# 66 TensorE passes of several shapes behind the last transposes of a hybrid decoder step

## The reference

```
proj = rmsnorm(x) @ w_in               # q, k, v, indexer, S5 input, two gates
y_a  = sparse_attention(...) @ w_attn_proj
y_b  = glu(gelu(s5_scan(u)) @ w_glu)
x    = x + (sigmoid(ga) * y_a + sigmoid(gb) * y_b) @ w_out
up   = rmsnorm(x) @ w_up               # 2 x 5632 columns
a    = silu(gate) * val                # after a causal depthwise conv of width 3
x    = x + a @ w_down
y    = rmsnorm(x)                      # the last norm; returned as y_prompt and y_sample
```

## Time and profile before

| | |
|---|---|
| time, median of 3 runs | 1541.68 us (1541.5 to 1542.19) |
| profiled execution, first to last instruction | 1540.4 us |
| TensorE busy with passes | 1528.9 us (99%) |
| TensorE busy with weight loads | 1513.1 us (98%) |
| VectorE, ScalarE, GpSimd busy | 1022.1, 665.2, 460.3 us |

### The profile page before, as it was taken

One profiled execution on the slowest core, in us unless ns is written; L12 is line 12 of the kernel. 1 busy time (PEld: TensorE's weight loads), 2 busy tenths in 40 slices (PEclk: granted clock), 3 DMA queues, 4 the chain that ended last, 5 costly groups with the idle time before them and its releaser, 6 DMA issues.

```text
span 1540.4 us, 33720 instructions
## 1 busy us (share of the span) xinstructions
PE 1528.9 (99%) x12448; PEld 1513.1 (98%) x12448; DVE 1022.1 (66%) x1477; ACT 665.2 (43%) x885; POOL 460.3 (30%) x581
## 2 busy tenths in 40 slices
PE   8999999999999999999999999999999999999998
PEld 8999999999999999999999999999999999999997
DVE  7655789888666676567676767777777764444443
ACT  6344345554666644444333333333333333333332
POOL 8993478867422101221111111111111100001100
PEclk9999999999999999999999999999999999999999
DMA  8896476776866586565554545454545465555552
GB/s 264 242 207 186 142 220 199 203 206 193 244 212 196 156 205 210 165 215 176 160 172 155 177 150 178 149 181 148 184 148 184 148 221 180 174 172 172 172 173 90
DMA packets 298942, 282.16 MB, mean 183 GB/s; under 512 B 35024, under 2 KB 290528, under 8 KB 298720
## 3 DMA queue, kind: packets, MB, share of 16 engines
q1 hardware_dynamic: 283008, 256.69, 55.5%
q10 hardware_dynamic: 13520, 16.62, 3.4%
q0 software_dynamic: 2320, 7.54, 1.5%
HBM read 266.73 MB, written 14.05 MB: 182 GB/s over the span
## 4 chain that ended last, share of the span: by engine, by line
PE 98%; DVE 0%; DMA 0%; SPq 0%; ACT 0%; issue 0%; DVEq 0%; ACTq 0%
PE banks L577 32%; PE banks L579 32%; PE banks L578 31%; PE banks L705 1%; PE banks L587 1%; PE banks L743 0%; PE banks L784 0%; DMA raw<-in_w_in 0%; PE banks L720 0%; PE banks L756 0%; PE banks L661 0%; PE banks L797 0%; PE banks L634 0%; PE banks L723 0%; DVE yo L1831 0%; PE banks L799 0%
## 5 line engine op out<-in xcount | busy, mean ns | idle before, releaser
L1292 DVE TENSOR_TENSOR wlo<-raw,whi 128x1024 fp32r<-128x1024 f32 x443 | 556.4, 1269 | 285.6 <-ACT whi L922 279.2
L922 ACT ACTIVATE whi<-raw 128x1024 fp32r<-128x1024 f32 x443 | 462.5, 1051 | 544.8 <-PE banks L579 500.4
L578 PE MATMUL banks<-h_lo,whi 128*128 128x288 f32 x1408 | 415.7, 295 | 0.0
L579 PE MATMUL banks<-h_hi,wlo 128*128 128x288 f32 x1408 | 415.7, 295 | 0.0
L577 PE MATMUL banks<-h_hi,whi 128*128 128x288 f32 x1408 | 414.6, 294 | 0.0
L577 PE MATMUL banks<-hhi,whi 128*128 128x288 f32 (+1 forms) x912 | 272.0, 298 | 2.4 <-DVE hlo L1318 2.4
L579 PE MATMUL banks<-hhi,wlo 128*128 128x288 f32 (+1 forms) x912 | 269.1, 295 | 0.0
L578 PE MATMUL banks<-hlo,whi 128*128 128x288 f32 (+1 forms) x912 | 268.9, 295 | 0.0
L578 PEld LDWEIGHTS banks<-h_lo,whi 128*128 128x128 f32 x1408 | 264.6, 188 | 0.1
L579 PEld LDWEIGHTS banks<-h_hi,wlo 128*128 128x128 f32 x1408 | 264.4, 188 | 0.0
L577 PEld LDWEIGHTS banks<-h_hi,whi 128*128 128x128 f32 x1408 | 264.1, 188 | 0.1
(11 more groups left out here) (354 smaller groups left out, 2166.3 us busy)
## 6 DMA issues: line engine op xcount, KB each, us to landing
raw<-in_w_up SPq DMA_DIRECT2D x352, 256.0 KB, 3.4
raw<-in_w_in SPq DMA_DIRECT2D x223, 256.0 KB, 3.5
raw<-in_w_down SPq DMA_DIRECT2D x176, 256.0 KB, 3.0
raw<-in_w_glu SPq DMA_DIRECT2D x64, 256.0 KB, 3.4
raw<-in_w_out SPq DMA_DIRECT2D x64, 256.0 KB, 3.3
raw<-in_w_attn_proj SPq DMA_DIRECT2D x32, 256.0 KB, 4.0
scratch_gates<-gt ACTq DMA_DIRECT2D x16, 288.0 KB, 3.9
gbt<-scratch_gates POOLq DMA_DIRECT2D x8, 288.0 KB, 3.7
```

What stands on the lines that cost most here:

```text
L578: pe.matmul(out, h, xl[:, kt, :], start=False, stop=False)
L579: mm = pe.matmul(out, lo, xh[:, kt, :], start=False, stop=kt == nk - 1)
L922: act.activation(whi[:, s, :, 0:cols], raw[:, s, :, 0:cols], ACT.Copy).then_inc(hi_ready, 1)
L1292: dve.tensor_tensor(wlo[:, s, :, 0:cols], raw[:, s, :, 0:cols], whi[:, s, :, 0:cols], ALU.subtract).then_inc(lo_ready, 1)
```

## The change

A buffer `plain` of 512 two-byte (bf16) columns is added. GpSimd fills it with 1.0 ahead of its first `squares` of the last stage and counts `consts_ready` to 3. Behind `y_tile(8)` TensorE waits until VectorE and ScalarE have taken steps 1 and 2 out of `acc[:, 2]` and `acc[:, 0]` and until `plain` is filled, and then runs eleven sets of six passes. Their operands are the weights left in `whi`, the activations left in `a_hi`, or `plain`; they write over `acc[:, 2]` (one set `acc[:, 2]` and `acc[:, 0]` in turn). Nobody reads what they write, and no semaphore is counted by them.

```diff
+    plain = at("plain", [P, 512], BF16, WK + 38016)
...
             y_tile(7)
             pe.wait_ge(sem("yo_ready1"), 1)
             y_tile(8)
+
+            def idle_passes(cols, rows=P, plain_type=False, banks_in_turn=False, at=0):
+
+                for k in range(6):
+                    bank = acc[0:rows, 2 - 2 * (k % 2) if banks_in_turn else 2, 0:cols]
+                    if plain_type:
+                        pe.matmul(bank, plain[:, 0:rows], plain[:, at:at + cols], start=True, stop=True)
+                    else:
+                        pe.matmul(bank, whi[:, k % 4, 0, 0:rows], a_hi[:, 20 + 2 * k:22 + 2 * k, :].rearrange("p k t -> p (k t)")[:, at:at + cols], start=True, stop=True)
+
+            pe.wait_ge(sem("yo_ready0"), 2)
+            pe.wait_ge(sem("yo_ready1"), 2)
+            pe.wait_ge(sem("consts_ready"), 3)
+            idle_passes(T)
+            idle_passes(512)
+            idle_passes(384)
+            idle_passes(256)
+            idle_passes(T, banks_in_turn=True)
+            idle_passes(T, rows=32)
+            idle_passes(T, at=2)
+            idle_passes(T, at=8)
+            idle_passes(T, plain_type=True)
+            idle_passes(512, plain_type=True)
+            idle_passes(T)
...
             for k in range(7):
                 pool.wait_ge(acc_free[1 - k % 2], 53 + k // 2 + k % 2)
+                if k == 0:
+                    pool.memset(plain[:, :], 1.0).then_inc(sem("consts_ready"), 1)
                 squares(x3, 2 * k, sq3, 9 + k)
```

## The result

The changed kernel takes 1545.14 us in the median of 13 runs (1544.47 to 1546.78), the kernel before 1541.9 us (1541.5 to 1544.28). The ratio is 1.0021 with a 95% interval of 1.0013 to 1.0028: 3.24 us slower, clear of no change, and on the line of 0.2% (3.1 us) that the prediction drew between "same" and "slower": the interval reaches from 2.0 to 4.3 us.

A forecast was written before the change was run, and what follows sets the result against it. TensorE bounds the kernel, busy 1528.9 of 1540.4 us; passes from 1532.77 add 10.06 us, 7.2 of the 10 us are hidden, and 2.85 on the median 1541.68 gives 1544.5 us, range 1543.6 to 1546.5.

The forecast's parts named there:

- line of 0.2%: Whole kernel: under 3.1 us (1544.8) counts as same; chances 0.68 same, 0.30 slower, 0.02 faster.
- The meeting: End of the blocks: engines meet only when TensorE has drained too; the span ends 0.2 us behind the last DRAIN.
- The room of 7.2 us: Behind the last transposes: TensorE comes to the meeting 7.2 us early, so added work is free up to that.
- The sum of the passes: Eleven added sets on TensorE: 10.06 us for 22,080 columns, bounds 9.20 and 10.20.
- The fixed 13 ns: Each added pass: 0.013 us over columns / 2.4 GHz at any width, rather than growing with the columns.
- The clock: During the added passes: 2.4 GHz throughout, since no gap comes before them.
- rival A: Added passes: clock not in full for part of them, 2.4 us more (1546.9), all low 1552.9; chance 0.09.
- B: Added sets: shifted, 32-weight-column or two-byte ones have another pace; shifted at half rate 1.3 us more, 1545.8; chance 0.10.
- C: Instruction supply for the passes: one more block behind y's transfers costs 1 to 2 us, 1545.5 to 1546.5; chance 0.05.
- D: End of kernel: nobody waits for the passes, or they overlap, all within the 7.2 us, 1541.7; chance 0.04.
- Added to the median: 1541.68 + 2.85: Kernel's end: span ends at 1543.25, 2.85 us over 1540.4; added to the median, 1544.5; forecast holds 0.70.
- The range: Whole time: 1543.6 to 1544.9 from the sum's bounds and spread of medians, reaching over B and C to 1546.5.

The follow-up runs named there:

- e2_twice: Changed kernel with the eleven sets standing twice, 132 passes: 1555.11 us beside 1542.44 for the kernel before (1.0085).
- e5_act_late: Kernel before, no passes, with eight unread ScalarE copies behind its last wait so that ScalarE ends last: 1544.06 us beside 1542.29 (1.0010).
- e9_first48: Changed kernel with only the first eight sets, 48 fp32r passes: 1542.95 us beside 1542.34 for the kernel before (1.0002).
- e8_places: Changed kernel with its sets replaced by eleven 288-column fp32r sets whose operands lie in different places: 1542.87 us, one run.
- e4_fill_only: Changed kernel with the fill of `plain` kept, the three waits and all passes removed: 1542.65 us beside 1542.44 for the kernel before (1.0001).
- e3_late: Changed kernel with the passes also waiting until the last of y_prompt has landed: 1555.16 us beside 1542.44 for the kernel before (1.0083).
- e7_widths: Changed kernel with its sets replaced by nine fp32r sets, one weight block and one moving operand, 256 to 512 columns: 1545.26 us, one run.
- e6_two_byte: Changed kernel with all eleven sets taking two-byte operands from `plain`, no shifts: 1544.43 us beside 1542.29 for the kernel before (1.0016).
- e1_first30: Changed kernel with only the first five sets, 30 passes: 1542.08 us beside 1542.44 for the kernel before (0.9999).

## Why the prediction was right, and where it was not

- **The meeting.** Right: TensorE's DRAIN waits for the last pass, and the span ends 0.2 us behind the last DRAIN. e2_twice and e5_act_late show it with more passes and with another engine.
- **The room of 7.2 us.** Right; e9_first48 fills it. It is the same in all eleven profiled executions, 7.1 to 7.3 us from the end of the last transpose to the end of SyncE's DRAIN, though both move together by 2 us: 1532.93 to 1540.18 before, 1532.07 to 1539.28 in e8_places, 1534.18 to 1541.35 in e4_fill_only.
- **When the passes start.** 1532.77 predicted, 1532.85 measured; the wait for the three counts cost nothing. Counted from the start of the last four transposes that is 0.36 and not 0.44: the first pass starts 0.03 behind the last transpose and not 0.11. In return it takes 215 ns to the next instead of 133, which the sum did not have (0.08).
- **The sum of the passes.** 10.06 predicted, 10.04 measured, by errors that cancel, which is luck: two-byte passes cost 10 ns less each (0.12 in all), the 512 and 384 sets 4 to 5 ns more each (0.05), the first distance 0.08 more. The two-byte kind does have a pace of its own, which the prediction named as a sign of being wrong; it was worth 0.12 us. The fixed 13 ns was the nearer choice; growth with the columns, the upper bound, does not hold.
- **The clock.** Right: 1.00 from the transposes to the end. The Trainium skill (TensorE: Matmul & The Clock Gate, Part 4) has transposes not engage it; here it stayed at 1.00 through 3.7 us of transposes (1529.40 to 1533.09). e3_late shows what rival A would have cost: 2.7 us for 6.1 us at the low level.
- **The fill.** Right, nothing; it takes 0.52 us of GpSimd's idle time (0.61 was the nearest row).
- **The rivals B, C and D.** The shifted sets take 2 ns more at most, no fetch of instructions held the passes, and nobody met without TensorE.
- **The end, "Added to the median: 1541.68 + 2.85".** Mechanism right, size off by a little. The span of the changed kernel came out as predicted (1543.25, measured 1543.3), to 0.05 us by luck, since the spans of its 13 executions go from 1542.6 to 1544.9. The mis-sized term is the baseline: the 1.28 us by which the median stood over the span. It is 1.76 to 1.95 us in every execution where time and span are known together, so the execution profiled before was 0.3 us slower than the median one; 1543.3 + 1.8 = 1545.1 is the measured median. The forecast of 1544.5 is therefore 0.6 low, of which 0.5 is this term.
- **The range.** The sum and the spread of the medians reached to 1544.9 only. The measured 1545.14 lies in the part of the range that was added for B and C, and neither happened: it is in the range by that allowance.
- **The difference.** 3.24 measured and 2.85 forecast cannot be told apart: 2.85 is a ratio of 1.0018, inside the interval. The kernel before stood at 1542.29 to 1542.44 in the medians taken beside the experiments, 0.4 to 0.5 over the 1541.9 of the result, and the changed kernel was not timed again beside those.
- **The line of 0.2%.** Placing the time "within 0.2%" rested on a margin of 0.23 us (3.08 for 0.2%, less 2.85), smaller than the error of the baseline: 0.18% predicted, 0.21% measured, with an interval that holds 0.20%. With the line that near, chances of 0.68 and 0.30 were too far apart.

## What to carry to other kernels

Work put behind an engine's last useful instruction is free up to the moment when the last other engine drains, and costs one for one beyond it; the end-of-block rows of each engine give that room at a glance. An experiment that hangs dummy work on the end of a kernel measures its own length less that room. When a forecast goes from a span to a median, take time and span of the same execution, or the error of the baseline is as large as the effect.

## What the runs showed of the hardware

At the high clock a stream of fp32r passes with a weight load each runs 10 to 19 ns slower for each pass than columns / 2.4 GHz, from 256 to 512 columns, whatever the number of weight columns (32, 72, 128), and with ones as with the kernel's own data; the same stream in bf16 runs 2.5 ns over it, and at the low clock fp32r has no surcharge. The kernel has about 11,000 such passes of 288 columns at 0.133 us: 0.010 us each are some 110 us of its 1542, an estimate by this count alone.

Executions of one kernel mostly differ by a microsecond or two (the 51 of the kernel before by 3.7 at most), and in the traces most of that is there within the first 40 us. In e7_widths the granted clock fell back to half for a stretch near the start, with TensorE at work throughout, while in the changed kernel it did not. Three stretches of e7_widths (busy us, passes, granted clock, DMA share, GB/s):

```profile
...
8.00:12.50 4.50, 2.39 (x18) 1.00 1.03 383
12.50:15.80 3.30, 3.30 (x16) 0.50 1.07 377
15.90:20.00 4.10, 4.10 (x33) 1.00 1.12 350
```

and the middle one in the changed kernel:

```profile
...
12.50:15.80 3.30, 3.30 (x27) 1.00 1.06 377
```

16 passes against 27 in 3.3 us. The stretch ahead has TensorE busy for about half of its 4.5 us; its one long gap, 2.1 us up to 11.62, ends with VectorE's `hlo`. e4_fill_only and e6_two_byte show the same fall. A stretch half idle does not decide it: in e1_first30 TensorE was busy for 2.08 of the same 4.5 us and in e5_act_late for 2.10, and the clock stayed at 1.00. `y_tile(7)` starts at 1532.8 to 1533.1 in the three executions with the fall, and at 1531.0 to 1532.5 in the eight without, so the fall comes with about 1 us, and 1.5 us of spread is there without it. The mean granted clock of each execution points the same way: of the changed kernel's 13, the ten at 1.000 have spans of 1542.6 to 1543.8 and the three at 0.999 of 1543.9, 1544.9 and 1544.9, and 3.3 us at half lower the mean by 0.001. Of the 51 of the kernel before, the 31 at 0.999 have a median span of 1540.3 and the 19 at 0.998 of 1541.3, with some overlap. No run changed the start of the program, so this goes together and is not shown as the cause; what lets the clock fall in some executions only stays open.
